# Indexer scores of a DSA layer: two heads at a time, in three passes of 64-row products, with three PSUM pairs in turn

## The reference, cut to what matters

```python
def block(args):                       # 128 query rows
    ql_b, qi_b, wi_b, start = args
    t = start + jnp.arange(Q_BLOCK)
    rel = jax.nn.relu(jnp.einsum('bthd,bsd->bths', qi_b, ki).astype(jnp.float32))
    iscore = jnp.einsum('bths,bth->bts', rel, wi_b.astype(jnp.float32))
    causal = s_idx[None, :] <= t[:, None]
    iscore = jnp.where(causal[None], iscore, -jnp.inf)
    _, sel = lax.top_k(iscore, topk)
...
    proj = h @ w_in[i]
    r_q, r_k, r_v, r_g, a_q, a_c, i_q, i_k, i_w = split_cols(proj)
    qi = i_q.reshape(B, S, IDX_HEADS, IDX_DIM)                 # 8 heads of 64
    ki = layer_norm(i_k, idx_k_norm_g[i], idx_k_norm_b[i])     # one key of 64 for all heads
```

## Time and profile before

| | before |
|---|---|
| median of 3 runs | 1431.39 us |
| lowest and highest | 1429.89 and 1433.33 us |
| the profiled execution | 1430.07 us |
| its span | 1428.3 us |
| PE busy | 1376.4 us (96%) |
| DVE busy | 1013.1 us (71%) |
| ACT busy | 605.1 us (42%) |
| POOL busy | 329.0 us (23%) |
| granted TensorE clock, mean | 0.995 |

### The profile page before, as it was taken

The page is one execution under the profiler, slowest core; times in us unless marked ns, Lnnn a source line. Parts: engine busy times, 40 slices in busy tenths (PEclk is TensorE's granted clock), DMA queues, the critical chain, the costliest instruction groups (busy, mean ns, idle before and its releaser), DMA issues.

```text
span 1428.3 us, 19391 instructions
## 1 busy us (share of the span) xinstructions
PE 1376.4 (96%) x7142; PEld 1125.8 (79%) x7142; DVE 1013.1 (71%) x1592; ACT 605.1 (42%) x1229; POOL 329.0 (23%) x383
## 2 busy tenths in 40 slices
PE   7999999999989889998999999999999999999998
PEld 7887888887777567777778888888887888888886
DVE  5748789998999546765877777777776765565633
ACT  6434552315823776574522222222222656453221
POOL 4545457711541475652000000000000000000000
PEclk9999999999999999999999999999999999999999
DMA  6322223225323021133234555444458866662211
GB/s 215 82 56 71 79 84 116 94 92 192 111 101 143 31 74 61 45 91 107 55 131 165 177 177 177 161 148 153 156 193 289 316 239 223 237 213 75 67 53 45
DMA packets 137150, 189.02 MB, mean 132 GB/s; under 512 B 12768, under 2 KB 75616, under 8 KB 137056
## 3 DMA queue, kind: packets, MB, share of 16 engines
q1 hardware_dynamic: 120224, 152.17, 32.5%
q10 hardware_dynamic: 16832, 35.61, 6.5%
HBM read 130.08 MB, written 57.67 MB: 131 GB/s over the span
## 4 chain that ended last, share of the span: by engine, by line
PE 79%; DVE 7%; issue 4%; ACT 4%; POOL 3%; DMA 1%; DVEq 1%; SPq 0%; ACTq 0%; POOLq 0%
PE ps L728 23%; PE ps L729 23%; PE ps L730 23%; PE ps L930 2%; PE ps L922 2%; PE ps L941 1%; PE ps L769 1%; POOL mxs L2721 1%; DMA raw<-in_w_in 1%; DVE sc L1915 1%; ACT lm L1444 1%; DVEq L1931 1%; PE ps L857 1%; PE ps L892 1%; PE ps L855 1%
## 5 line engine op out<-in xcount | busy, mean ns | idle before, releaser
L2593 POOL TENSOR_TENSOR smf<-smf,sml 128x1 f32<-128x1 f32 x16 | 9.1, 579 | 739.3 <-DVE smf L2474 625.2
L728 PE MATMUL ps<-bh,ah 128*128 128x512 f32 x308 | 120.1, 390 | 2.4 <-DVE u2b L2315 2.4
L730 PE MATMUL ps<-bh,al 128*128 128x512 f32 x308 | 119.9, 389 | 0.0
L729 PE MATMUL ps<-bl,ah 128*128 128x512 f32 x308 | 119.8, 389 | 0.0
L728 PE MATMUL ps<-wbh,xth 128*128 128x512 f32 (+1 forms) x320 | 118.9, 371 | 0.0
L729 PE MATMUL ps<-wbl,xth 128*128 128x512 f32 (+1 forms) x320 | 117.7, 368 | 0.0
L730 PE MATMUL ps<-wbh,xtl 128*128 128x512 f32 (+1 forms) x320 | 117.7, 368 | 0.0
L2421 DVE TENSOR_TENSOR al<-ra,ah 128x512 fp32r<-128x512 f32 x77 | 53.1, 690 | 70.7 <-ACT ah L1671 70.3
L728 PE MATMUL ps<-th,ssh 128*128 128x512 f32 x240 | 93.6, 390 | 1.8 <-DVE u2b L2291 1.2
L730 PE MATMUL ps<-th,ssl 128*128 128x512 f32 x240 | 93.4, 389 | 0.0
L729 PE MATMUL ps<-tl,ssh 128*128 128x512 f32 x240 | 93.4, 389 | 0.0
(11 more groups left out here) (375 smaller groups left out, 3871.1 us busy)
## 6 DMA issues: line engine op xcount, KB each, us to landing
raw<-in_w_in SPq DMA_DIRECT2D x49, 256.0 KB, 3.0
wt<-in_w_ffn_down SPq DMA_DIRECT2D x44, 256.0 KB, 7.2
down_sums<-wt ACTq DMA_DIRECT2D x44, 256.0 KB, 5.0
ra<-hidden_sums SPq DMA_DIRECT2D x44, 256.0 KB, 2.9
rb<-down_sums SPq DMA_DIRECT2D x44, 256.0 KB, 3.5
raws<-in_w_ffn_gate SPq DMA_DIRECT2D x21, 512.0 KB, 3.9
raws<-in_w_ffn_up SPq DMA_DIRECT2D x21, 512.0 KB, 5.3
ret_rows<-stg SPq DMA_DIRECT2D x32, 320.0 KB, 3.4
```

The lines of the kernel that those rows point to most:

```text
L728: pe.matmul(o, ah, wh, start=start, stop=False, skip_group_check=resumes)
L729: pe.matmul(o, ah, wl, start=False, stop=False, skip_group_check=resumes)
L730: return pe.matmul(o, al, wh, start=False, stop=stop, skip_group_check=resumes)
```

## The change

Scores are made for two heads at a time. The high and low parts of the queries get tiles of their own, `IQH` and `IQL`, with two heads per tile on the two halves of the partitions, as the projection leaves them. So ScalarE's copy and VectorE's subtraction are one instruction of 128 partitions each where there were two of 64. `indexer_scores` is called for even n only and makes heads n and n+1: for each 512 keys, three passes (qh*kh, ql*kh, qh*kl), each of two 64-row matmuls, one on the upper and one on the lower half. Head n uses PSUM pair 1 + n%3, so three pairs go in turn, and the count of block 4 that wrote into pair 3 writes to an SBUF tile `JUNK4`. The call for n still waits for head n-2 to be added.

```diff
-    QS = sb("qs", [P, H, QW], 148, F32R)
+    IQH = sb("iqh", [P, NP, QW], 148, F32R)
+    IQL = sb("iql", [P, NP, QW], 160, F32R)
...
+    JUNK4 = sb("junk4", [P, (B0 + 3) * P], 207, mybir.dt.uint8)
...
         def indexer_scores(n):
 
-            b, h = B0 + n // H, n % H
+            b, m = B0 + n // H, n % H // 2
             if n == 0:
                 pe.wait_ge(s["v_kl"], 1)
-            if n >= 2:
+            else:
                 pe.wait_ge(s["v_acc"], n - 1)
-            keys = (b + 1) * P
+            keys, qs = (b + 1) * P, slice((b - B0) * P, (b - B0 + 1) * P)
             for k0 in range(0, keys, 512):
                 k1 = min(k0 + 512, keys)
-                for key in (KH, KL):
-                    m = pe.matmul(pair(1 + n % 2)[:, k0:k1], QS[:, h, (b - B0) * P:(b - B0 + 1) * P], key[:, k0:k1],
-                                  start=(key is KH), stop=(key is KL))
-            m.then_inc(s["t_ix"], 1)
+                for i, (q, key) in enumerate(((IQH, KH), (IQL, KH), (IQH, KL))):
+                    for h, j in enumerate(HALF):
+                        ins = pe.matmul(pair(1 + (n + h) % 3)[:, k0:k1], q[j, m, qs], key[j, k0:k1], start=(i == 0),
+                                        stop=(i == 2))
+            ins.then_inc(s["t_ix"], 2)
...
                 if todo and k in (1, 4, 7):
-                    indexer_scores(todo.pop(0))
+                    n = todo.pop(0)
+                    if n % 2 == 0:
+                        indexer_scores(n)
...
             if c == 1:
-                for h, j in enumerate(HALF):
-                    ins = sc.copy(QS[j, 2 * m + h, query_cols(g)], bank(g % 2, unit_width(g))[j, :])
+                ins = sc.copy(IQH[:, m, query_cols(g)], bank(g % 2, unit_width(g)))
...
-            o = pair(1 + n % 2, (B0 + n // H + 1) * P)
+            o = pair(1 + n % 3, (B0 + n // H + 1) * P)
...
-            for h, (j, i) in enumerate(zip(HALF, HALF[::-1])):
-                q = QS[:, 2 * (g % 4) + h, query_cols(g)]
-                ins = v.tensor_tensor(q[i, :], bank(g % 2, unit_width(g))[j, :], q[j, :].bitcast(F32), ALU.subtract)
-            ins.then_inc(s["v_qlo"], 1)
+            v.tensor_tensor(IQL[:, g % 4, query_cols(g)], bank(g % 2, unit_width(g)),
+                            IQH[:, g % 4, query_cols(g)].bitcast(F32), ALU.subtract).then_inc(s["v_qlo"], 1)
...
         def count_junk(b):
-            return JUNK3[:, :] if b == B0 + 1 else pair(3, (b + 1) * P)
+            return (JUNK3, JUNK4)[b - B0 - 1][:, :]
```

More of the change, by code:

```diff
@@ L1910, in add_head @@
             b, h = B0 + n // H, n % H
-            o, sc_b = pair(1 + n % 2, (b + 1) * P), SC[b - B0][:, :]
+            o, sc_b = pair(1 + n % 3, (b + 1) * P), SC[b - B0][:, :]
             dve.wait_ge(s["a_rl"], n + 1)
```

## The result

The kernel with heads in pairs takes 1434.2 us (median of 22 runs, 1432.2 to 1436.1); the kernel before, run beside it, 1431.0 (22 runs). The ratio is 1.0020, interval [1.0014, 1.0027]: slower, by just about what can be told from no change. A second comparison gives 1434.4 against 1431.0, 1.0023 [1.0014, 1.0032], and the kernel before against itself 1.0003. The forecast was 1430.9, half a microsecond less than before, with "no change" likeliest. The measured time lies inside the range, but it moved the other way: 3.2 us more.

The account below looks back on a forecast made before the run. TensorE, busy 96% of the span, was taken as the bound, except VectorE from 105 to 137 us. Scores and waits +0.8, queries -1.2, taken as -0.5 us in all: median 1430.9 us, range 1426.5 to 1434.5.

Parts of the forecast that it names:

- Change 1: Paired 64-row scores on TensorE: three passes for four, but 0.41 us per call for switching; +2.1 us on its queue.
- Change 2: Fewer TensorE waits for VectorE's adds between 113 and 137 us: 1.3 us of waits on the matmuls go.
- Change 3: Merged query copy and subtraction of 128 partitions: waits in the query units shrink, unit 12 starts 1.2 us earlier.
- nothing in the rows speaks against it: Query units: said of the full gain's condition, that VectorE and ScalarE instructions of 128 partitions cost as much as of 64.
- The prediction's own sign of being wrong: Query units: the forecast is wrong if unit 12 still starts at 58.4 us instead of near 57.2.
- rival 3: Query units: the gain is lost because another normalisation step is late; +0.8 us, 1432.2 us, chance 0.06.
- Change 4: Third PSUM pair and the count into SBUF: tenths per count stay under VectorE's idle time; no further wait removed.
- The sum: Whole kernel: +0.8 - 1.2 = -0.4 us, taken as -0.5 for shed matmul spacing.
- It is carried to the end: After the projection: the -0.5 us lasts to the kernel's end, since retention starts from TensorE's last unit.
- Rivals 1 and 2: TensorE's score switch costs little or nothing, 1424.7 us, chance 0.17; or costs 0.70 us per call, 1436.9 us, chance 0.13.

Follow-up runs that it names:

- two_excursions: Changed kernel with each pair's scores for 640 keys and more split over two places of a unit, 16 more visits to 64-row products; 1443.2 us, ratio 1.0086.
- three_pairs: Kernel before, old 128-row heads one at a time, but three PSUM pairs in turn and block 4's count in SBUF; 1430.6 us, ratio 0.9994.
- pool_later: Changed kernel with one more wait on GpSimd, so two of its subtractions start only after the third query subtraction; 1432.4 us, ratio 1.0006.
- no_excursion: Changed kernel with three 128-row passes per pair instead of 64-row products, odd heads' products left out, for timing alone; 1430.9 us, ratio 0.9997.
- three_pairs_pool_later: Kernel before with three PSUM pairs in turn and the later GpSimd subtractions, no 64-row scores or merged query copy; 1429.7 us, ratio 0.9987.
- Four_heads: Changed kernel with four heads instead of two per call for blocks of 384 and 512 keys; 1433.0 us, ratio 1.0007.
- split_queries: Changed kernel with the query copy and subtraction again in two halves of 64 partitions each; 1435.3 us, ratio 1.0030.

## Why the prediction was right or wrong

**Change 1, right.** The forecast had 0.41 per call, the traces show 0.40, and each size's cost is within 0.03; two_excursions shows the same 0.40 for an added excursion. All calls together were put at +2.1; three pairs against the changed kernel gives +2.4, 0.3 of it late first matmuls.

**Change 2, right, with more hidden than said.** 1.5 us of waits went (1.3 forecast). Changes 1 and 2 together are +0.9 in units 15 to 31, against +0.8.

**Change 3, wrong in size.** The step that failed is "nothing in the rows speaks against it": VectorE's chain came 0.39 earlier (53.08 - 22.10 and 53.36 - 22.77 after the last matmul of unit 0), but ScalarE's weight copy, now behind two cheaper query copies, came 0.95 earlier, and GpSimd's subtraction with it, into VectorE's way. Of 1.2 us came 0.39. The prediction's own sign of being wrong came true: unit 12 starts at 58.7 and not near 57.2. This is rival 3, to which I gave 0.06; it had its sign in the trace, GpSimd's 3.18 us for two where 1.29 is usual for one. Removing the meeting gives 1.3 more (pool_later).

**Change 4, right.** A count of block 4 takes 875 ns with its output in SBUF and 883 with PSUM.

**The sum.** The projection came out at +0.5 instead of -0.5, and the whole of that 1.0 is change 3 (0.8) and the rest of change 1 and 2 (0.1 to 0.2).

**The step that decided: "It is carried to the end".** It is not. After the projection the changed kernel loses 1.3 us in a wait before the down projection that the prediction did not look at. The change adds 80 matmuls and 80 weight loads to TensorE's instructions, so their 16 KB loads fall elsewhere. That moving them changes the wait is shown by both kernels with added waits, in both directions (3.7 to 2.9, 2.4 to 4.1), by one trace each. How is open. The load may delay the stores by sharing a DMA engine or queue with them; this is only argued, from the load's place inside the 1.49 us that one of the four issues took. Against it, two_excursions has the load among the stores, a usual 1.99 us for their issues and still 4.1 us of wait, and no_excursion has the load 1.5 us ahead of the stores and 3.3 us of wait.

The lower clock, 0.0013 per run, goes with 0.9 us: 0.5 + 1.3 + 0.9 = 2.7 of the 3.2 measured; the rest is not placed. What sets the clock is open. A stretch at 1.2 GHz at this entry is in 12 of the 14 traces; it starts up to 1.6 us ahead of the first matmul there or up to 1.5 behind it, and it makes the first 24 matmuls 1.5 to 2.6 us slower. It is missing in the kernel before and in three_pairs, after waits of 2.4 and 2.3, but three_pairs_pool_later has it after 2.3. Four_heads with 4.1 us of wait has a mean clock of 0.995. No run here separates the clock from the change.

**Rivals 1 and 2** both fell: no call of 1024 keys takes 1.4 or above 2 us. The page "TensorEngine Tiling (Array Packing)" of the Trainium skill, section Key Properties, says that a change of tiling mode drains TensorE, and the 0.09 in and 0.09 to 0.10 out agree with it. The "up to 2x" of its section Theoretical Speedup is not reached between long full-array products: a pair of heads of 512 keys takes 1.09 us instead of 0.91.

## What to carry to other kernels

Work out row packing per visit: here a visit to 64-row products costs 0.40 us, as much as 1.8 passes of 512 columns, so it pays only if a visit saves more than that, and if the engine that takes the results has room. A small gain on one engine that starts another's work earlier must be read against the third engine that this one can hold up: here ScalarE's earlier copy let GpSimd start before VectorE. And a change of 160 instructions in the longest stream shifted all later instruction loads: repeat a 0.1 to 0.2% result with padded streams before putting it down to the edit.

## What the runs showed of the hardware that I had not expected

- TensorE's instructions come in 16 KB packets, one each 27 to 29 us in the long products. Adding 96 waits to TensorE alone moved them 6 us earlier, 160 waits 9 us. With a packet 1.0 to 1.9 us behind the start of a burst of stores, five of six traces show 2.5 to 3.3 us for the four issues, where 1.95 to 2.2 is usual, and TensorE waits 3.3 to 4.1 us twenty us later; with the packet 4.9 to 8.0 us ahead it waits 2.3 to 3.3.
- A VectorE step of 8 columns (L1879) took 1.10 instead of 0.17 us beside GpSimd's subtraction.
- Over 95 executions of the kernel before, 0.001 less mean clock went with 0.7 us more, half of what 0.001 of 1430 us would be. Part of the time at 1.2 GHz lies where TensorE waits: in split_queries a stretch of 6.8 us begins 1.6 us before the wait at the down projection ends.
- 128-column passes in pairs of 64 rows start every 0.11 us, but three cost 0.68 when they stand alone.
